# Two weight buffers moved by 32 and 96 bytes in a streaming-encoder block, one core

## The reference

```python
mod = (silu(c) @ ada_w + ada_b).reshape(9, 1024)      # sh1 sc1 g1 sh2 sc2 g2 sh3 sc3 g3
h = modulate(rmsnorm(x, norm_ffn1_g), sh1, sc1)
x = x + 0.5 * g1 * (silu(h @ w1) * (h @ w3)) @ w2      # 1024 -> 2816 -> 1024
h = modulate(rmsnorm(x, norm_mix_g), sh2, sc2)
xb, xc, xu, cq, ckv, kr = split(h @ w_in)              # 1024 -> 2240
y_a = xb * causal_conv3(xc * xu)                       # 512 channels
y_b = mla(cq, ckv, kr, positions)                      # 4 heads, chunks of 64 tokens
x = x + g2 * (concat(groupnorm(y_a), headnorm(y_b)) @ w_out)
h = modulate(rmsnorm(x, norm_ffn2_g), sh3, sc3)
x = x + 0.5 * g3 * (silu(h @ w1b) * (h @ w3b)) @ w2b
out = rmsnorm(x, final_norm_g)
```

## Time and profile before

| | |
|---|---|
| three runs | 1031.13, 1031.44, 1033.59 us; median 1031.44 |
| the profiled execution | 1033.02 us |
| its span, first to last instruction | 1031.4 us |
| granted TensorE clock, mean | 0.99 |
| PE, PEld, DVE, ACT busy | 98%, 80%, 51%, 39% |

### The profile page before, as it was taken

One profiled execution on the slowest core, in us unless ns is written; L12 is line 12 of the kernel. 1 busy time (PEld: TensorE's weight loads), 2 busy tenths in 40 slices (PEclk: granted clock), 3 DMA queues, 4 the chain that ended last, 5 costly groups with the idle time before them and its releaser, 6 DMA issues.

```text
span 1031.4 us, 13364 instructions
## 1 busy us (share of the span) xinstructions
PE 1006.6 (98%) x4587; PEld 824.1 (80%) x4587; DVE 523.9 (51%) x705; ACT 400.4 (39%) x571; POOL 57.8 (6%) x82
## 2 busy tenths in 40 slices
PE   6999999999999999999999999999999999999997
PEld 3478888888888888788887887788888888888886
DVE  2777877778753333644366525643344434423332
ACT  5253443443442222431255633444344443422322
POOL 2210110111000000000000310000000000000000
PEclk9899999999999999999999999999999999999998
DMA  9566876678533324133221112133332333233232
GB/s 337 181 210 202 260 223 210 201 240 252 175 92 95 96 89 117 51 82 101 72 77 41 42 42 82 41 104 99 102 98 86 101 102 92 86 97 100 88 107 82
DMA packets 179000, 127.82 MB, mean 124 GB/s; under 512 B 5424, under 2 KB 166002, under 8 KB 178976
## 3 DMA queue, kind: packets, MB, share of 16 engines
q1 hardware_dynamic: 170544, 97.92, 31.8%
q0 software_dynamic: 8432, 29.58, 8.8%
HBM read 125.39 MB, written 2.10 MB: 124 GB/s over the span
## 4 chain that ended last, share of the span: by engine, by line
PE 95%; DVE 2%; ACT 1%; issue 1%; DMA 1%; POOL 0%; DVEq 0%; ACTq 0%; POOLq 0%
PE pb L769 88%; PE pb L882 1%; PE pb L806 1%; PE pb L1071 1%; DVE hl L1250 1%; DVE ubuf L1257 1%; DMA vec<-in_conv_w_dram 1%; PE pb L813 0%; PE pb L788 0%; PE pb L1051 0%; PE pb L897 0%; PE pb L892 0%; PE pb L1020 0%; ACT wh L418 0%; PE pb L1031 0%
## 5 line engine op out<-in xcount | busy, mean ns | idle before, releaser
L769 PE MATMUL pb<-hh,wh 128*128 128x512 f32 x912 | 359.6, 394 | 6.1 <-DVE hl L1250 2.0
L769 PE MATMUL pb<-hh,wl 128*128 128x512 f32 x912 | 356.7, 391 | 0.0
L769 PE MATMUL pb<-hl,wh 128*128 128x512 f32 x912 | 356.5, 391 | 0.0
L1218 DVE TENSOR_TENSOR wl<-raw,wh 128x1024 fp32r<-128x1024 f32 x156 | 191.1, 1225 | 279.0 <-ACT wh L418 279.0
L418 ACT ACTIVATE wh<-raw 128x1024 fp32r<-128x1024 f32 x163 | 172.6, 1059 | 412.4 <-PE pb L769 412.4
L769 PEld LDWEIGHTS pb<-hh,wh 128*128 128x128 f32 x912 | 172.0, 189 | 47.5 <-DVE hl L1250 4.6
L769 PEld LDWEIGHTS pb<-hh,wl 128*128 128x128 f32 x912 | 172.1, 189 | 36.0
L769 PEld LDWEIGHTS pb<-hl,wh 128*128 128x128 f32 x912 | 172.3, 189 | 34.8
L769 PE MATMUL pb<-gh,wh 128*128 128x512 f32 x352 | 137.0, 389 | 0.0
L769 PE MATMUL pb<-gh,wl 128*128 128x512 f32 x352 | 136.9, 389 | 0.0
L769 PE MATMUL pb<-gl,wh 128*128 128x512 f32 x352 | 136.9, 389 | 0.0
(11 more groups left out here) (214 smaller groups left out, 705.2 us busy)
## 6 DMA issues: line engine op xcount, KB each, us to landing
raw<-in_ffn_w_dram SPq DMA_DIRECT2D x104, 512.0 KB, 3.9
ada_ring<-in_ada_w_dram POOLq DMA_DIRECT2D x56, 512.0 KB, 5.1
raw<-in_ffn_w_dram SPq DMA_DIRECT2D x32, 448.0 KB, 3.4
raw<-in_w_in_dram SPq DMA_DIRECT2D x17, 512.0 KB, 3.9
ada_start<-in_ada_w_dram SPq DMA_DIRECT2D x16, 512.0 KB, 9.9
raw<-in_w_out_dram SPq DMA_DIRECT2D x8, 512.0 KB, 3.4
x_nat<-in_x_dram SPq DMA_DIRECT2D x4, 512.0 KB, 5.4
out_dram<-o_nat SPq DMA_DIRECT2D x8, 256.0 KB, 2.9
```

The lines of the kernel that those rows point to most:

```text
L769: last = pe.matmul(o, a, b, start=start and j == 0 and t == 0, stop=stop and j == len(pairs) - 1 and t == 2)
L1218: dve.tensor_tensor(wl[par][:, :], raw[par][:, :], wh[par][:, :].bitcast(F32), ALU.subtract).then_inc(lo_ready, 1)
```

## The change

Three tiles that nothing uses are placed around the two buffers of the weights' remainders: 32 bytes ahead of `wl0`, 64 bytes between `wl0` and `wl1`, 160 bytes behind `wl1`. The three add up to 256, so what lies behind is 256 bytes further on, and all but `wl0` and `wl1` keep their distance from the activations up to a multiple of 256. No instruction is added, removed, moved or changed in shape.

```diff
         hl = at("hl", [P, DT, SEQ], F32R)
         raw = [at(f"raw{b}", [P, UW]) for b in range(2)]
         wh = [at(f"wh{b}", [P, UW], F32R) for b in range(2)]
-        wl = [at(f"wl{b}", [P, UW], F32R) for b in range(2)]
+        at("off_first", [P, 8])
+        wl0 = at("wl0", [P, UW], F32R)
+        at("off_second", [P, 16])
+        wl1 = at("wl1", [P, UW], F32R)
+        at("off_third", [P, 40])
+        wl = [wl0, wl1]
         kst = at("kst", [P, K_COLS + 2])
```

## The result

| | before | after |
|---|---|---|
| median of four runs | 1032.29 us | 1052.32 us |
| lowest to highest | 1031.13 to 1033.59 | 1051.09 to 1053.02 |
| profiled execution, span | 1033.02, 1031.4 | 1052.11, 1050.2 |

The four of before are the three known ahead of the prediction and one more of 1033.13 us.

What follows compares the result with a forecast made beforehand. The prediction took the number of matmuls times the interval between their starts as the bound. Only the `wl` loads cost: 1296 x 8 ns = 10.4 us on the 1031.4 us span, giving a median of 1042 us, range 1024 to 1055.

Steps and rivals of the forecast that it cites:

- by which door the change comes in: Matmul stream: an edit of addresses can act only through the interval between starts; a nanosecond on each is 3.9 us.
- (1): Everything behind `wl1`: moving it by 256 bytes costs nothing.
- (2): VectorE's writes of `wl` at the new addresses: taken as nothing, covered by 279.0 us of waiting for `wh`.
- (4): `v_unit`: 8 matmuls have `wl` as the moving operand; 8 of some 3900 can't matter.
- The term of 8 ns per load of `wl`: TensorE's loads of `wl` under streaming matmuls: 1296 loads at 8 ns each, 10.4 us more, priced from the `sacc` rows.
- rival A: Matmul stream never back in its beat: 5.3 ns on every interval, +20.6 us, 1052; chance 0.20.
- One row that spoke for less: 384-column matmul on `exact` over a load of `sacc`: stays with its neighbour at a mean of 336 ns, price about 0.
- The period of 64 bytes: Distance of load from stream: effect assumed to repeat every 64 bytes, so 160, 32 and 96 all leave 32.
- The prediction's warning: `wl` buffers: with a period above 64 bytes, 32 and 96 may be harmless or differ, and every second unit be slower.
- Rival B: Loads of `wl`: the change costs nothing, as stream and load might be coupled by time alone; 1031.4, chance 0.22.
- Rival C: Matmul of `wh` and `hl`: faster, as the new distance fits better; 1029 down to 1014, chance 0.22.

Runs made afterwards that it cites:

- the kernel with one buffer of two: Against the kernel before, only `wl0` was moved by 32 bytes, with `wl1` at 0; 1047.67 us, against 1032.3 for the kernel before.

## Why the prediction was wrong

**What bounds the kernel, and by which door the change comes in: right.** What moved is the interval between the starts of matmuls. The durations of loads and subtractions, TensorE's waits and the intervals at the half clock are the same. Steps (1), (2) and (4) of the change, at nothing, held. For (1): in the kernel with one buffer of two, `wl1` lies 256 bytes further on and `gh` 512, and the units of `wl1` run at 389 ns. For (2): VectorE's 1225 ns stayed, the wait for `wl` is 1.1 us. (GpSimd subtracts seven units, not five, which changes nothing.) For (4): the eight matmuls that stream `wl` went from 390 to 394 ns.

**The term of 8 ns per load of `wl` was mis-sized.** It measured 17.1 ns over the 512 loads of the long stretch. The 8 ns were read correctly: the matmul over the load of `sacc` has 397 against 389 ns, and the interval over the isolated load is 235 against 227. But they are only the first interval of a disturbance of four. The `sacc` row could not show the rest, because behind it came eight matmuls of one column, not a stream. That disturbances last stands in the earlier trace rows, and I used it for rival A alone, instead of asking how much of such a tail any single disturbance must carry. With the tail, 1296 x 17.1 = 22.2 us, against 20.0 measured; the span grew by 18.8. 0.9 us of the difference is start-up: the first stretch of 144 begins at 59.97 us before and at 59.03 after. And 17.1 ns are the price in the long stretch alone; a stretch of 144 like the one of 33.59 us above took before

```profile
258.55 32.90 PE pb L769 x144
```

which is 0.69 us for 48 loads, 14.4 ns each. Just behind its break the intervals were long before as well.

One row that spoke for less was misread. The 336 ns of the earlier trace rows are a mean of two; a window that holds only the matmul over the load of `sacc` shows 337, so the other has 334, and by the starts its interval is 176 against 173 ns:

```profile
L813 PE MATMUL pb<-exact 128*128 128x384 f32 x1 | 0.3, 337 | 0.0
```

**Rival A had the size, and its reason only in half.** It took 5.3 ns per interval; 5.7 was measured. It said that the stream never finds its beat again, since it has two matmuls and needs five. The runs show something else: at a distance of 32 an isolated load costs 19.5 ns, and a load in every block 19.9, so for this one pattern the price per load is the same whether there is time to recover or not. And with a displaced load in every block the stream has a beat, of 0.70 us per block. The agreement of 15.9 and 17.1 ns per block is partly luck.

**The period of 64 bytes was an assumption, and wrong.** 64 and 128 cost 13.3 ns per block. The multiples of 256 are free as far as rows of before and these runs go, 16 bytes are free for an isolated load, and everything in steps of 32 between costs 13 to 20. That 160 was taken to stand for 32 was right by luck too: both cost 20.0. The prediction's warning came about in part. 32 and 96 both cost, but not the same, and in the change every second unit is slower: 700.0 ns per block with `wl0` at 32, 695.8 with `wl1` at 96.

**Rival B and the rule behind it.** The Trainium skill, SBUF — State Buffer, § Who interferes with whom, has TensorE's two read ports independent and waiting on nobody. The runs disagree with what that would make of the time: one load read 32 bytes further on lengthens the interval above it by 8 ns and costs 20 in all, in a kernel where nothing else is changed but an offset of 16 bytes in other units. **Rival C** found no distance in steps of 32 that is faster.

**What stays open.** Which reads meet where. Shown is that distances decide and not places (all tiles moved: nothing), that loads all alike but away from the streams are slow, and that loads which all fit the streams above them are still slow when the streams, and the two operands of a product, differ among themselves. Why one block out of step costs 53 or 33 ns where one in every block costs 13.3 or 16.6 is open. That the cause is a collision in the memory's parts is argued, from the half clock and the 32-byte grain, and not shown. Nor is it known whether the 13.4 ns of surplus that every interval has at distance 0 are of the same kind.

## What to carry to other kernels

In a stream like this one, of fp32r matmuls at the full clock with a load for each, keep the stationary and the moving operands at the same remainder by 256 bytes, every one of them, and check that after any edit that adds a small tile in front of them. A kernel whose time changes by one or two per cent after such an edit should be judged by the interval between matmul starts over a long uninterrupted stretch, where 0.1 us is legible. And when a disturbance is priced from a single row, ask what would have followed it in the stream: the row right behind a disturbance is not its whole cost.

## What the runs showed of the hardware that I had not expected

A displacement by 32 bytes of the stationary operand of one matmul in three costs 2.6% (1030.72 to 1057.0 us), and one of 16 bytes nothing that can be seen in the isolated load. The prices take few values: 0, 13.3, 15.8, 16.6 and 20 ns per block where all blocks of a unit are alike, and 20, 33, 40 and 53 for isolated ones. One displaced load in a block, and all three, have the same price (358.65 and 358.66 us). At the half clock there is none: starts 0.43 us apart with and without the displacement.
